# A hybrid encoder block on one core: halved projection blocks, earlier K, seven output tiles ahead of the Toeplitz products

## The reference, cut to what matters

```
u = rmsnorm(h);  z = u @ W_in                         # 1024 -> 1024
a = pool_mixer(z[:, :512])     # 4 groups: (window mean - z) @ pool_w, windows 2, 4, 8, 16
s = ssm_mixer(z[:, 512:])      # 32 groups x 16 channels, 64 complex states, both directions, GELU, GLU
h = h + concat(a, s) @ W_out
h = h + hierarchical_moe(rmsnorm(h))                  # 4 x 8 experts, two per token
h = h + sigmoid(rmsnorm(h) @ W_g + b_g) * (p @ W_ple)
out = rmsnorm(h)
```

## Time and profile before

| | us |
|---|---|
| three runs, median (lowest, highest) | 601.13 (596.47, 601.69) |
| the profiled execution's own time | 599.62 |
| its span | 597.9 |
| PE busy | 500.0 (84%) |
| DVE busy | 237.1 (40%) |
| POOL busy | 158.4 (26%) |
| ACT busy | 150.9 (25%) |
| mean granted TensorE clock | 0.909 |

### The profile page before, as it was taken

One profiled execution on the slowest core, in us unless ns is written; L12 is line 12 of the kernel. 1 busy time (PEld: TensorE's weight loads), 2 busy tenths in 40 slices (PEclk: granted clock), 3 DMA queues, 4 the chain that ended last, 5 costly groups with the idle time before them and its releaser, 6 DMA issues.

```text
span 597.9 us, 6989 instructions
## 1 busy us (share of the span) xinstructions
PE 500.0 (84%) x2649; PEld 289.7 (48%) x2649; DVE 237.1 (40%) x641; ACT 150.9 (25%) x247; POOL 158.4 (26%) x136
## 2 busy tenths in 40 slices
PE   4797968997689999449999996898688888779993
PEld 3343667463347446435555553455454454344441
DVE  4698783999102326622222221221112111143444
ACT  6232332146333212100111111110111012402454
POOL 1089994450222000013222222212201011001450
PEclk9798975998899999758999999988989889969997
DMA  8862100049814692925999999999999998530011
GB/s 310 161 125 61 34 0 1 1 148 222 86 71 195 242 420 98 407 79 195 417 419 420 417 417 419 422 420 418 422 419 419 422 407 339 224 139 1 0 70 70
DMA packets 53950, 142.85 MB, mean 239 GB/s; under 512 B 27504, under 2 KB 32636, under 8 KB 40988
## 3 DMA queue, kind: packets, MB, share of 16 engines
q1 hardware_dynamic: 48620, 133.89, 59.9%
q0 software_dynamic: 4896, 8.47, 3.9%
q10 hardware_dynamic: 400, 0.04, 0.0%
HBM read 136.57 MB, written 14.19 MB: 252 GB/s over the span
## 4 chain that ended last, share of the span: by engine, by line
PE 75%; DVE 9%; issue 5%; DMA 5%; ACT 3%; SPq 2%; POOLq 0%; DVEq 0%
PE bank L1349 69%; DVE ring L722 3%; PE bank L1600 3%; DMA ring<-k_d 2%; PE bank L1614 1%; PE bank L1546 1%; DVE bank L722 1%; DMA h<-in_x_dram 1%; DVE ut L722 1%; DMA k_d<-ring 1%; SPq L404 1%; DMA moe<-v_d,gidx_all 1%; DVE moe L722 1%; SPq L397 1%; PE bank L1416 1%
## 5 line engine op out<-in xcount | busy, mean ns | idle before, releaser
L1349 PE MATMUL bank<-ring,moe 128*64 128x256 f32 (+3 forms) x1136 | 157.9, 419 | 24.8 <-issue 14.9
L1349 PEld LDWEIGHTS bank<-ring,moe 128*64 128x64 f32 (+1 forms) x1136 | 99.4, 158 | 67.4 <-issue 35.1
L1278 POOL DMA_INDIRECT pairs_d<-ut,sidx_all x32 | 31.9, 996 | 182.6 <-ACT ut L472 115.2
L722 DVE TENSOR_TENSOR moe<-moe,bank 64x128 f32<-64x128 f32 x64 | 18.6, 291 | 145.3 <-ACT moe L653 144.3
L1349 PE MATMUL bank<-ut,big 128*128 128x512 f32 x128 | 62.8, 652 | 3.4 <-ACT ut L484 3.4
L1349 PE MATMUL bank<-ring,ut 128*128 128x512 f32 x128 | 58.0, 613 | 1.4 <-DVE ut L722 1.4
L1349 PE MATMUL bank<-big,moe 128*64 128x256 f32 (+1 forms) x280 | 50.0, 446 | 10.8 <-issue 8.5
L1349 PE MATMUL bank<-big,ut 128*128 128x512 f32 x128 | 57.5, 607 | 1.5 <-DMA big<-in_w_out_dram 1.5
L653 ACT ACTIVATE moe<-bank 64x256 f32<-64x256 f32 x32 | 12.1, 377 | 178.2 <-PE bank L1349 178.2
L1349 PEld LDWEIGHTS bank<-ut,big 128*128 128x128 f32 x128 | 26.6, 212 | 36.0 <-issue 32.4
L1349 PEld LDWEIGHTS bank<-big,moe 128*64 128x64 f32 x280 | 28.1, 150 | 27.0 <-issue 14.7
(11 more groups left out here) (167 smaller groups left out, 524.6 us busy)
## 6 DMA issues: line engine op xcount, KB each, us to landing
ring<-in_exp_w_gate_dram SPq DMA_DIRECT2D x22, 1024.0 KB
ring<-in_exp_w_up_dram SPq DMA_DIRECT2D x22, 1024.0 KB
ring<-in_exp_w_down_dram SPq DMA_DIRECT2D x22, 1024.0 KB, 26.9
big<-in_exp_w_gate_dram SPq DMA_DIRECT2D x10, 1024.0 KB
big<-in_exp_w_up_dram SPq DMA_DIRECT2D x5, 1024.0 KB
big<-in_exp_w_down_dram SPq DMA_DIRECT2D x5, 1024.0 KB
zbuf<-in_exp_w_up_dram SPq DMA_DIRECT2D x5, 1024.0 KB
zbuf<-in_exp_w_down_dram SPq DMA_DIRECT2D x5, 1024.0 KB
```

What stands on the lines that cost most here:

```text
L722: return dve.tensor_tensor(o, a, b, op)
L1278: pool.indirect_dma_start(pairs, bass.IndirectOffsetOnAxis(ap=index, axis=0), at(ut, ALL, k * 512, [[1, 512]]), None, bounds_check=4 * T - ...
L1349: return pe.matmul(o, a, b, start=start, stop=stop, skip_group_check=loose)
```

## The change

- PE: `win` takes a function `between` that is called after the fourth of its 8 products. Lambda's transposes go between the halves of `win(0)`; `w_rows(b)` becomes `w_rows(b, hb)`, one half of W at a time, of which one goes between the halves of blocks 2 and 3 of the state space and of `z_pool(0)` and `z_pool(1)`, and the other behind them. `z_pool(1)` moves ahead of `end_states(2)`. K moves ahead of `z_pool(3)` and needs only two pooling blocks copied out. `wout0(0)` to `wout0(6)` all stand ahead of the Toeplitz products.
- The fourth set of end states uses banks 4 and 5 instead of 6 and 7, so it waits for two sets copied out, not three; `K_BANK` changes with it.
- ACT: the powers' copies to bank 2 go ahead of C's; the copies of W, of the end states and of the pooling blocks follow PE's new order; the GELU table is loaded earlier; `xo_out(0)` and `zp_out(3)` come behind K's copies.
- DVE: `e_out(1)` comes before the padded copy of B, which is finished (`kb_done`) before `e_out(2)`.
- SP: the load of the second half of W_out goes behind the Toeplitz reads.

```diff
--- before.py
+++ after.py
@@ -276,9 +276,10 @@
         ident = at(cst, ALL, C_ID, [[1, P]])
         ident32 = at(cst, (0, 32), C_ID, [[1, 32]])
 
-        B_PIN, B_TMP, B_WT, B_E = 2, 3, 4, 6
+        B_PIN, B_TMP, B_WT = 2, 3, 4
+        E_BANK = (6, 6, 6, 4)
         PS_A2, PS_T1, PS_T2 = 0, 4 * G, 6 * G
-        K_BANK = (4, 5, 6, 7, 2, 0)
+        K_BANK = (2, 1, 6, 7, 4, 5)
         Y_BANK, A_BANK = (0, 1, 2, 4), (5, 6, 7)
         YT_BANK, G_BANK = (3, 0, 5, 1), (2, 4, 7, 6)
         XO_CUT = (0, 12, 24, 36, 48, 58, NCH)
@@ -384,9 +385,6 @@
                 sp.wait_ge(zs_stored, 16 * GB * (m + 1))
                 sp.dma_start(at(ring, ALL, R_U + m * T, [[1, T]]),
                              dr(z_d, m * T, [[G * NCH, P], [1, T]])).then_inc(u_ready[m], 16)
-            sp.wait_ge(zp_ps, NB)
-            sp.dma_start(at(big, ALL, 4 * DM, [[DM, 4], [1, DM]]),
-                         dr(A["w_out"], 4 * P * DM, [[DM, P], [P * DM, 4], [1, DM]])).then_inc(ld_wout1, 16)
             sp.wait_ge(k_ps, 6)
             sp.dma_start(at(big, ALL, 0, [[DM, 4], [1, DM]]),
                          dr(A["w_out"], 0, [[DM, P], [P * DM, 4], [1, DM]])).then_inc(ld_wout0, 16)
@@ -404,6 +402,9 @@
                 sp.dma_start(at(ring, (CH * s, CH * s + CH), R_T, [[P, G], [1, P]]),
                              dr(k_d, (L - 1 - s) * CH, [[15 * CH, CH], [CH * 15 * CH, G], [1, P]])
                              ).then_inc(toep_ready, 16)
+            sp.wait_ge(zp_ps, NB)
+            sp.dma_start(at(big, ALL, 4 * DM, [[DM, 4], [1, DM]]),
+                         dr(A["w_out"], 4 * P * DM, [[DM, P], [P * DM, 4], [1, DM]])).then_inc(ld_wout1, 16)
             sp.wait_ge(tu_done, 1)
             sp.dma_start(at(ring, ALL, R_GLU, [[DP, 4], [1, DP]]),
                          dr(A["glu_w"], 0, [[DP, P], [P * DP, 4], [1, DP]])).then_inc(ld_glu, 16)
@@ -524,33 +525,31 @@
                      at(bank[m % 2], ALL, 0, [[L, NCH], [1, L]]), zs_done)
 
             zs_out(0)
-            act.wait_ge(c_ps, 1)
-            act.activation(at(ring, ALL, R_CL, [[1, 512]]), bank[4][:, :], ACT.Copy).then_inc(c_done, 1)
-            act.activation(at(ring, ALL, R_CL + 512, [[1, 512]]), bank[5][:, :], ACT.Copy, scale=-1.0
-                           ).then_inc(c_done, 1)
-            act.activation(at(vec, ALL, V_POOL, [[1, 12]]), bank[6][:, 0:12], ACT.Copy).then_inc(vec_done, 1)
-
             act.wait_ge(pow_done, 1)
             for ri in range(2):
                 pw = R_PW + ri * 9 * G
                 copy(at(bank[B_PIN], FWD, ri * L * G, [[G, L], [1, G]]),
                      at(ring, FWD, pw + 7 * G, [[-G, L], [1, G]]), pin_done)
                 copy(at(bank[B_PIN], BWD, ri * L * G, [[1, L * G]]), at(ring, BWD, pw, [[1, L * G]]), pin_done)
-
-            def wt_out(b):
-
-                for hb in range(2):
-                    act.wait_ge(wt_ps, 2 * b + hb + 1)
-                    if b >= 2:
-                        act.wait_ge(e_ps, b - 1)
-                    for ri in range(2):
-                        copy(at(moe, ALL, M_WT + (b % 2) * 2048 + ri * 1024 + hb * 512, [[1, 512]]),
-                             bank[B_WT + ri][:, :], wt_done)
+            act.wait_ge(c_ps, 1)
+            act.activation(at(ring, ALL, R_CL, [[1, 512]]), bank[4][:, :], ACT.Copy).then_inc(c_done, 1)
+            act.activation(at(ring, ALL, R_CL + 512, [[1, 512]]), bank[5][:, :], ACT.Copy, scale=-1.0
+                           ).then_inc(c_done, 1)
+            act.activation(at(vec, ALL, V_POOL, [[1, 12]]), bank[6][:, 0:12], ACT.Copy).then_inc(vec_done, 1)
+
+            def wt_out(b, hb):
+
+                act.wait_ge(wt_ps, 2 * b + hb + 1)
+                if b >= 2:
+                    act.wait_ge(e_ps, b - 1)
+                for ri in range(2):
+                    copy(at(moe, ALL, M_WT + (b % 2) * 2048 + ri * 1024 + hb * 512, [[1, 512]]),
+                         bank[B_WT + ri][:, :], wt_done)
 
             def e_out(b):
 
                 act.wait_ge(e_ps, b + 1)
-                src = bank[B_E]
+                src = bank[E_BANK[b]]
                 copy(at(ring, FWD, R_X + 64 + b * GB, [[1, GB], [64, NCH]]),
                      at(src, FWD, 0, [[NCH, GB], [1, NCH]]), e_done)
                 copy(at(ring, BWD, R_X + 64 * NCH + b * GB, [[1, GB], [-64, NCH]]),
@@ -572,41 +571,53 @@
                          at(ring, BWD, R_X + 64 * (b - 1), [[1, 2 * G], [-64, b - a]]), xo_bwd)
 
             zs_out(1)
+            wt_out(0, 0)
             zs_out(2)
-            wt_out(0)
+            wt_out(0, 1)
+            wt_out(1, 0)
             zs_out(3)
-            wt_out(1)
+            wt_out(1, 1)
             e_out(0)
+            wt_out(2, 0)
+            wt_out(2, 1)
             zp_out(0)
-            wt_out(2)
             e_out(1)
-            wt_out(3)
+            wt_out(3, 0)
+            wt_out(3, 1)
+            zp_out(1)
             e_out(2)
             e_out(3)
-            zp_out(1)
+            warm(2, ACT.Gelu_apprx_tanh)
             zp_out(2)
-            xo_out(0)
-            zp_out(3)
 
             act.wait_ge(wt_ps, 2 * NB)
             for k in range(6):
                 n = 3 * 9 * CH if k < 5 else 9 * CH
                 act.wait_ge(k_ps, k + 1)
                 copy(at(ring, ALL, R_K + k * 27 * CH, [[1, n]]), bank[K_BANK[k]][:, 0:n], k_done)
-            xo_out(1)
-            warm(2, ACT.Gelu_apprx_tanh)
-            for i, m in enumerate(ZP_ORDER):
+
+            def a_out(i):
+
+                m = ZP_ORDER[i]
                 act.wait_ge(a_ps, i + 1)
                 act.activation(at(ut, ALL, m * T, [[1, T]]), bank[A_BANK[i % 3]][:, :], ACT.Copy, scale=vcol(V_POOL + m)
                                ).then_inc(a_done, 1)
+
+            xo_out(0)
+            zp_out(3)
+            for i in range(3):
+                a_out(i)
+            xo_out(1)
+            a_out(3)
 
             def wo0_out(n):
                 act.wait_ge(wo0_ps, n + 1)
                 least(act, wo0_done, n - 1)
                 copy(at(moe, ALL, M_PT + (n % 2) * 512, [[1, 512]]), bank[A_BANK[n % 3]][:, :], wo0_sb)
 
+            wo0_out(0)
             xo_out(2)
-            for n in range(4):
+            for n in range(1, 4):
                 wo0_out(n)
             xo_out(3)
             wo0_out(4)
@@ -838,7 +849,7 @@
             def e_out(b):
 
                 dve.wait_ge(e_ps, b + 1)
-                src = bank[B_E + 1]
+                src = bank[E_BANK[b] + 1]
                 dve.tensor_copy(at(ring, FWD, R_X + 64 + G + b * GB, [[1, GB], [64, NCH]]),
                                 at(src, FWD, 0, [[NCH, GB], [1, NCH]])).then_inc(e_done, 1)
                 dve.tensor_copy(at(ring, BWD, R_X + 64 * NCH + G + b * GB, [[1, GB], [-64, NCH]]),
@@ -870,6 +881,7 @@
                 if b == NB - 2:
                     e_out(0)
 
+            e_out(1)
             dve.memset(grid(R_X, [[1, 64]]), 0.0).then_inc(x_zero, 1)
             seq(dve.tensor_copy(at(bank[B_TMP], ALL, PS_A2, [[1, 4 * G]]), at(small, ALL, S_A2, [[1, 4 * G]])))
             dve.wait_ge(win_ps, NB)
@@ -877,13 +889,13 @@
             bb = [[R_BBI - R_BB, 2], [CH, G], [1, CH]]
             own.do(dve.memset(at(big, FWD, B_KB + CH, kb), 0.0))
             own.do(dve.memset(at(big, BWD, B_KB, kb), 0.0))
-            e_out(1)
+            own.settle()
             own.do(dve.tensor_copy(at(big, FWD, B_KB, kb), at(ring, FWD, R_BB, bb)))
             own.do(dve.tensor_copy(at(big, BWD, B_KB + CH, kb), at(ring, BWD, R_BB, bb)))
+            own.settle()
+            dve.tensor_copy(at(big, ALL, B_KB + 2 * CH, kb), grid(R_BB, bb)).then_inc(kb_done, 1)
             e_out(2)
-            dve.tensor_copy(at(big, ALL, B_KB + 2 * CH, kb), grid(R_BB, bb)).then_inc(kb_done, 1)
             e_out(3)
-            own.settle()
             dve.wait_ge(x_zero, 1)
             dve.wait_ge(e_done, 16)
             lanes = bank[B_TMP]
@@ -1352,10 +1364,12 @@
                 return at(ring, parts, off, [[1, n]])
 
 
-            def win(m, dst, col):
+            def win(m, dst, col, between=None):
 
                 order = (1, 3, 5, 7, 0, 2, 4, 6)
                 for j in order:
+                    if between and j == order[4]:
+                        between()
                     last = mm(bank[dst][:, :], at(big, ALL, col + j * DP + m * P, [[1, P]]),
                               at(ut, ALL, j * T, [[1, T]]), j == order[0], j == order[-1])
                 return last
@@ -1369,12 +1383,15 @@
             last.then_inc(turned_ps, 1)
             pe.wait_ge(ut_done, KC)
             pe.wait_ge(ld_win0, 16)
-            win(0, 0, 0).then_inc(win_ps, 1)
-
-            pe.wait_ge(lam_done, 1)
-            for k, src in enumerate((12, 13, 14, 15)):
-                last = pe.transpose(bank[7][:, k * G:(k + 1) * G], lam(src), ident32)
-            last.then_inc(lam_ps, 1)
+
+            def lam_turned():
+
+                pe.wait_ge(lam_done, 1)
```

(70 more changed lines are left out.)

## The result

The changed kernel takes 566.66 us (median of four runs, 566.1 to 568.34) against 599.05 in the same comparison: a ratio of 0.9459, 95% interval 0.9429 to 0.9489. The profiled execution took 568.34 us, the kernel before 599.62: 31.3 less, where the prediction had said 32.3 less. That execution was the slowest of the changed kernel's four, so its profile shows a little less gain than the medians do (32.4).

The account below looks back on a forecast made before the run. PE's idle time and low clock were taken as the bound: 24.0 us idle and 14 of low clock go, 3.0 + 0.9 + 1.7 come back, so 32.3 us less, forecast 568, range 560 to 580.

Parts of the forecast that it names:

- five idle pieces: PE's remaining idle time before the change, put around the copies of W and of the end states.
- Lambda earlier: Lambda's transposes inside block 0: DVE's powers, B and W start 3.5 us earlier; PE doesn't wait.
- step 4: ACT's powers' copies before C's: POOL loses 1.9 us, `CW` ready at 88.8, costing nothing while cover lasts.
- Projection and W: Between projection blocks: W's first half ready at 40.0, waits of 2.83 and the like go, slack 0.5 at first.
- End states: The four sets of end states wait for nothing; K can start at 94.2.
- named bounds: Stated uncertainties, among them POOL's first difference beside the scan, 1.4 faster to 3 slower; together 564 to 576.
- K, the last block, the pause: K 94.2 to 102.3, `z_pool(3)` until 109.3; PE idles 3 us for POOL's last difference, tiles start at 116.9.
- Seven tiles: Output tiles ahead of the Toeplitz products: 24.0 us plus 1.7 for the clock, ending at 142.6.
- Toeplitz x U and y_rows: Behind the tiles: Toeplitz x U 3.6 us, `y_rows` 7.2 without waiting, ending at 153.4.
- The first rival: Transposes hold the clock down in the interleaved stretch, 37.0 to 94.2: end at 626; chance 0.04.
- The second rival: DVE and POOL set the pace, at W's halves or POOL's chain before the tiles: 572 to 585; chance 0.14.
- The third: Order changes but the end doesn't, through late Toeplitz reads or expert stream: 595 to 605; chance 0.04.

Follow-up runs that it names:

- before_c_behind: The kernel before, with only ACT's copies of C put behind those of the powers: 597.36 us, ratio 0.9957 to the kernel before.
- lam_late: The changed kernel with lambda's four transposes back behind the whole of block 0: 568.75 us, ratio 0.9486 to the kernel before.
- c_first: The changed kernel with ACT's copies of C ahead of the powers' copies again: 564.73 us, ratio 0.9423 to the kernel before.
- w_behind: The changed kernel with both halves of W turned behind whole blocks, lambda's transposes still inside block 0: 567.39 us, ratio 0.9469 to the kernel before.
- junk: The changed kernel with five thrown-away products in PE's pause, four before the last pooling product and one behind: 563.95 us, ratio 0.9419 to the kernel before.
- tiles_old: The changed kernel with four output tiles ahead of Toeplitz x U and three behind it: 570.36 us, ratio 0.9517 to the kernel before.
- filled: The changed kernel with three output tiles begun in PE's pause, before the last pooling product: 558.58 us, ratio 0.9327 to the kernel before.
- states_old: The changed kernel with the second pooling block behind the fourth end states and all sets in one bank pair: 579.51 us, ratio 0.9678.
- front_old: The changed kernel with lambda late, W behind whole blocks and the second pooling block behind the end states: 582.56 us, ratio 0.9717.

## Why the prediction was right

The sum, 32.3, measured 31.25 in the profile and 32.4 by the medians. (Its last step has a slip: 567.3 and 1.5 are 568.8, not 568; and of the five idle pieces that it puts around copies four are that, 7.4 us, and one is 0.43 before the pooling products.) By its steps:

1. *Lambda earlier.* Said 3.5 us, and DVE did start 3.9 earlier (25.06 against 28.92). But W's first half was ready at 37.3, not 40.0: the powers took 3.35 instead of 5.49. The missing 2.1 us are the lock shown in `before_c_behind`. The rows for it stood in the trace before, and I had costed the edit (step 4) for POOL alone.
2. *Projection and W.* No wait before any half. The slack was 2.7, not the 0.5 that I called thin, and `lam_late`, with DVE 2.65 later, costs PE only 0.65 there. A half of W turned takes 0.87 beside products, not 0.97.
3. *End states.* Right in kind, all waits gone; K at 92.22, not 94.2: eight halves at 0.1 less are 0.8, six blocks 0.5, four sets 0.3 and block 0's end 0.4.
4. *POOL.* `CW` ready at 88.45 (said 88.8), the last difference at 113.58 (said 115.0); the first one took 8.1 beside the scan where it took 9.25 beside DVE's large copies. That was one of the named bounds.
5. and 6. *K, the last block, the pause.* Right in place and cause: 3.39 us of idle time ended by POOL's last difference, then 0.87 for ACT (said 3 and 0.9). The sum had the last block's copy out 0.5 us before POOL was free for it; it was 1.0 before (108.03, and POOL's next operation at 109.14). The rest of the pause is that block's own way, as `c_first` and `w_behind` show.
7. *Seven tiles.* Here the size was off. Said 24.0 + 1.7, found 27.28; the last pooling product took 2.08, said 0.87. That is 4.5 us over 24.0 and 0.87, not 1.7; of it 0.3 is a tile's own price (24.27 at full clock in `junk`) and 4.2 the clock. I had taken the price of before, where the pause was 2.43 and 1.46 us; here PE was busy 2.82 of 7.08 us. `junk` gives 3.9 back in its profile and 2.7 in time. The price itself varies: `tiles_old`, with the same pause, lost 1.5 us less.
8. *Toeplitz x U and y_rows.* 3.54 and 7.16 (said 3.6 and 7.2), behind the seventh tile without a wait.

K 2.0 early and the tiles 2.8 dearer nearly cancel: that the total came closer than its terms is luck. What I costed at nothing (the moved load, the splits, the rest of the program) cost nothing: 412.16 and 412.21.

The first rival, transposes that hold the clock down, is out: a granted 1.00 over 84.5 us with eight groups of them in between, each at full speed (0.87 us). The Trainium skill (TensorE: Matmul & The Clock Gate, Part 4) says that transposes don't count as busy; spaced this way they have no price in the trace, and no run here has longer rows of them. The second rival, that DVE and POOL set the pace, is true in a small part: POOL is behind at one place, by 1 us, and that place was in the sum. The third is refuted by the result.

What the prediction had no word on is how the parts cover for each other. Undone singly they cost 0 to 1 us (K), 0 to 4 (tiles), 1.6 to 2 (lambda), 0 to 1 (halves) and 10 to 13 (states): 12 to 21 of 31. For K and the tiles the pair shows the cover (8 to 10 together). How much of the rest is cover and how much belongs to edits that no run undoes is open: DVE's new order around the padded copy of B, the GELU table's place, `xo_out(0)` behind K's copies and the later load of W_out's second half were not run by themselves.

## What to carry to other kernels

Add up an engine's idle time and the extra time of its work at the low clock over the stretch that sets the end: that is about what a reordering can give. Here it was 24 and an estimated 14 us. The changed order took 31 of these 38; `filled`, with PE busy at full clock throughout, took 40 (138.20 for 178.53), so the estimate was a little low. When a pause stays, look at what stands behind it in the queue that is ready already; three tiles begun without their last product turned 8.7 us of pause and low clock into work. Edits that cover for each other cost little when they are undone one at a time: undo them in pairs too.

## What the runs showed of the hardware

DVE's small products of two state buffer inputs lost some 2.1 us to two POOL sums of 1.3 us (5.49 for 18 products against 3.35). A pause in which PE was busy 2.82 of 7.08 us cost 4.2 us in clock besides its 4.26 of idle time: 2.08 instead of 0.87 for one product and 27.28 instead of 24.27 for seven tiles, part of them at 1.2 GHz. In another execution (`tiles_old`) the same pause cost the tiles 1.5 us and not 3.0. Of two waits of 2.54 us at the same place in the order, one was followed by a set of end states in 6.38 us (`states_old`) and one by a set in 3.68 (`front_old`). Eight groups of eight transposes among blocks and half blocks left the clock at 2.4 GHz.
